# Making the first layer's shift and scale by quarters of the channels

## The reference

```python
c_act = jax.nn.silu(c)
for l in range(DEPTH):                                   # DEPTH = 2
    mod = c_act @ w_ada[l] + b_ada[l]                    # (1, 3 * 2048)
    shift, scale, gate = jnp.split(mod, 3, axis=-1)
    h = _rmsnorm(x, norm_g[l]) * (1.0 + scale[:, None, :]) + shift[:, None, :]
    z = h @ w_in[l]                                      # 13 pieces of 512 columns
    ...                                                  # mixers, gates
    x = x + gate[:, None, :] * (concat @ w_out[l])
...                                                      # pooling layer, latent attention layer
```

## Time and profile before

| | |
|---|---|
| median of 3 runs | 2161.24 us (2158.2 to 2162.18) |
| profiled execution, its own time | 2157.21 us |
| span of the profiled execution | 2155.4 us |
| TensorE busy | 2087.6 us, 97% of the span |
| VectorE, ScalarE busy | 1513.2 us, 948.2 us |
| DMA | 511.40 MB, mean 237 GB/s |

### The profile page before, as it was taken

How to read it: one execution, slowest core, us unless ns; L and a number is a source line. 1 busy time by engine, 2 the same in 40 slices (tenths; PEclk the granted TensorE clock), 3 DMA queues, 4 the chain that set the end, 5 groups by cost and what they waited for, 6 DMA issues and landing times.

```text
span 2155.4 us, 32744 instructions
## 1 busy us (share of the span) xinstructions
PE 2087.6 (97%) x13530; PEld 1762.3 (82%) x13530; DVE 1513.2 (70%) x1923; ACT 948.2 (44%) x1318; POOL 201.7 (9%) x386
## 2 busy tenths in 40 slices
PE   5889999999999999999999999999999999999997
PEld 3668878887889878886987878787778999988876
DVE  0355879886765888865897868678788886455554
ACT  2234555553535555555632222223247553444452
POOL 2211110110011111110010100000100000000000
PEclk9999999999999999999999999999999999999999
DMA  9998887779697787777576646555887778322253
GB/s 381 383 332 304 276 315 245 251 270 343 201 356 265 263 274 264 256 270 275 184 275 201 212 146 196 163 174 166 299 289 256 233 255 265 103 70 77 78 191 131
DMA packets 215484, 511.40 MB, mean 237 GB/s; under 512 B 19728, under 2 KB 26096, under 8 KB 213680
## 3 DMA queue, kind: packets, MB, share of 16 engines
q1 hardware_dynamic: 155536, 297.83, 40.8%
q0 software_dynamic: 54464, 201.76, 26.9%
q10 hardware_dynamic: 5344, 9.84, 1.5%
HBM read 500.93 MB, written 8.43 MB: 236 GB/s over the span
## 4 chain that ended last, share of the span: by engine, by line
PE 70%; DVE 7%; DMA 4%; ACT 2%; issue 1%; DVEq 0%; ACTq 0%
PE ps L821 21%; PE ps L822 20%; PE ps L823 20%; DMA w_raw<-in_w_out 3%; DVE ada_acc L2306 2%; PE ps L877 2%; PE ps L1500 1%; DVE wl L2406 1%; DVE wl L2413 1%; PE ps L1492 1%; ACT wh L1604 1%; PE ps L1483 1%; DMA ada_raw<-in_ada_w 0%; PE ps L1199 0%; PE ps L1019 0%
## 5 line engine op out<-in xcount | busy, mean ns | idle before, releaser
L2413 DVE TENSOR_TENSOR wl<-w_raw,wh 128x1024 fp32r<-128x1024 f32 x280 | 334.7, 1221 | 197.9 <-ACT wh L1604 197.1
L1604 ACT ACTIVATE wh<-w_raw 128x1024 fp32r<-128x1024 f32 x280 | 291.6, 1056 | 346.9 <-PE ps L823 234.4
L1656 ACT ACTIVATE wh<-w_raw 128x1024 fp32r<-128x1024 f32 x220 | 230.5, 1057 | 403.2 <-PE ps L823 346.9
L821 PE MATMUL ps<-hh,wh 128*128 128x256 f32 x1280 | 371.5, 290 | 9.8 <-DVE hl L2474 9.0
L822 PE MATMUL ps<-hh,wl 128*128 128x256 f32 x1280 | 361.2, 282 | 0.0
L823 PE MATMUL ps<-hl,wh 128*128 128x256 f32 x1280 | 360.7, 282 | 0.0
L2406 DVE TENSOR_TENSOR wl<-w_raw,wh 128x1024 fp32r<-128x1024 f32 x220 | 266.8, 1221 | 130.6 <-ACT wh L1656 130.2
L821 PE MATMUL ps<-act_hl,wh 128*128 128x256 f32 (+1 forms) x1056 | 351.4, 333 | 2.9 <-DVE wl L2406 2.9
L822 PE MATMUL ps<-act_hl,wl 128*128 128x256 f32 (+1 forms) x1056 | 348.6, 330 | 0.0
L823 PE MATMUL ps<-act_hl,wh 128*128 128x256 f32 (+1 forms) x1056 | 348.4, 330 | 0.0
L2306 DVE SCALAR_TENSOR_TENSOR ada_acc<-ada_raw,cpad,ada_acc 128x1024 f32<-128x1024 f32 x263 | 329.5, 1280 | 13.5 <-DMA ada_raw<-in_ada_w 11.7
(11 more groups left out here) (414 smaller groups left out, 3113.0 us busy)
## 6 DMA issues: line engine op xcount, KB each, us to landing
ada_raw<-in_ada_w POOLq DMA_DIRECT2D x272, 512.0 KB, 5.3
w_raw<-in_w_in SPq DMA_DIRECT2D x208, 512.0 KB, 5.3
w_raw<-in_pool_in SPq DMA_DIRECT2D x72, 512.0 KB, 4.7
w_raw<-in_w_out SPq DMA_DIRECT2D x64, 512.0 KB, 7.6
w_raw<-in_mla_in SPq DMA_DIRECT2D x56, 512.0 KB, 4.8
ada_fourth<-in_ada_w POOLq DMA_DIRECT2D x48, 512.0 KB, 6.6
w_raw<-in_pool_out SPq DMA_DIRECT2D x48, 512.0 KB, 5.5
w_raw<-in_mla_out SPq DMA_DIRECT2D x32, 512.0 KB, 3.8
```

What stands on the lines that cost most here:

```text
L821: pe.matmul(dst, ah, bh, start=start, stop=False, skip_group_check=True)
L1604: act.activation(wh[:, g % RING, :], w_raw[:, g % RING, :], ACT.Copy).then_inc(w_hi, 1)
L1656: act.activation(as_raw(g, wh[:, r, :]), raw_of(g), ACT.Copy).then_inc(w_hi, 1)
L2413: dve.tensor_tensor(wl[:, g % RING, :], w_raw[:, g % RING, :], wh[:, g % RING, :].bitcast(F32), ALU.subtract).then_inc(w_lo, 1)
```

## The change

The early blocks become 128 rows by 512 columns of shift and the same 512 columns of scale, so sixteen blocks finish both for a quarter of the channels. The order of the first three pieces follows the quarters: two slots each of pieces 0 and 1 for the first quarter (g = 0 to 3), two each for the second (4 to 7), four of piece 2 (8 to 11), two of each piece for the third (12 to 17) and for the fourth (18 to 23). The early blocks are spread anew between the slots, SyncE loads only blocks 1 to 15 of them, its weight loads get gates on the number of used blocks (`EARLY_GATE`), all eight `turn_x` stand in the first sixteen blocks, VectorE's first sixteen later blocks move from steps 0 to 12 into steps 5 to 12, TensorE's from steps 4 to 10 into steps 5 to 10, and `tab` and the slabs are loaded behind slots 22 and 26.

```diff
-SLAB_SLOTS = ({20: 2, 24: 2}, {116: 2, 120: 2})
+SLAB_SLOTS = ({22: 2, 26: 2}, {116: 2, 120: 2})
-EARLY_PIECES = (0, 2, 1, 3)
+EARLY_Q = GRP // P
+EARLY_FROM = (0, 4, 12, 18)
+EARLY_SPLIT = (4, 4, 4, 0)
+EARLY_TILL = ((22, 24, 26, 28), (37, 38, 39, 40, 41, 42, 43, 44), (53, 54, 55, 56, 57, 58))
+EARLY_GATE = {1: 8, 2: 14, 4: 24, 6: 30, 12: 40, 14: 46, 18: 56, 20: 62}
...
-SLOTS_OF = [[(p, s) for s0 in (0, HALF) for p in range(3) for s in range(s0, s0 + HALF)]
+SLOTS_OF = [[(p, s) for p in range(2) for s in (0, 1)] + [(p, s) for p in range(2) for s in (2, 3)]
+            + [(2, s) for s in range(4)] + [(p, s) for s0 in (4, 6) for p in range(3) for s in (s0, s0 + 1)]
...
-EARLY_STEPS = [RING, 2]
+EARLY_STEPS = [RING + 1, 2]
...
-ADA_DVE = [{**spread(0, 0, [1] * 8 + [2, 1, 2, 1, 2]), **spread(1, 13, [1, 2, 1, 2, 2, 2] + [1] * 6),
+ADA_DVE = [{**spread(0, 5, [2] * 8), **spread(1, 13, [1, 2, 1, 2, 2, 2] + [1] * 6),
...
-ADA_PE = [{**spread(2, 4, [1, 2, 2, 2, 3, 3, 3]), **spread(4, 12, [4] + [3] * 4), **spread(5, 19, [2] * 8)},
+ADA_PE = [{**spread(2, 5, [2, 2, 3, 3, 3, 3]), **spread(4, 12, [4] + [3] * 4), **spread(5, 19, [2] * 8)},
...
-            eng.dma_start(early_bufs[r], ada_k[:, 0, i % ADA_SLOTS, piece * ADA_W:(piece + 1) * ADA_W]
-                          ).then_inc(early_here(i)[0], 16)
+            eng.dma_start(early_bufs[r].rearrange("p (j n) -> p j n", j=2),
+                          ada_k[:, 0, i % ADA_SLOTS, 0:2, at:at + GRP]).then_inc(early_here(i)[0], 16)
...
-            for i in range(1, 2 * ADA_SLOTS, 2):
+            for i in range(1, ADA_SLOTS, 2):
                 early_load(sp, i)
...
-                    if l == 0 and g in (1, 3 * HALF):
-                        sp.wait_ge(ada_pe, 52 if g > 1 else 29)
+                    if l == 0 and g in EARLY_GATE:
+                        sp.wait_ge(ada_pe, EARLY_GATE[g])
...
             for n in range(4, 8):
                 turn_x(n)
-                early_slots(2 * n, 2 * n + 2)
-            ada_turn(0, 6)
-            early_slots(ADA_SLOTS, ADA_SLOTS + 6)
-            pe.wait_ge(ada_row, 5)
+                early_slots(n + 4, n + 5)
+            pe.wait_ge(ada_row, 4)
             for n in range(4):
                 turn_x(n)
-                early_slots(ADA_SLOTS + 6 + 2 * n, ADA_SLOTS + 8 + 2 * n)
-            early_slots(2 * ADA_SLOTS - 2, 2 * ADA_SLOTS)
-            ada_turn(1, 7)
+                early_slots(n + 12, n + 13)
...
+                        if l == 0 and g in EARLY_FROM:
+                            n = EARLY_FROM.index(g)
+                            if n:
+                                early_slots(EARLY_TILL[n - 1][-1], ADA_SLOTS * (n + 1))
+                            ada_turn(n, 6 + n % 2)
+                            early_slots(ADA_SLOTS * (n + 1), ADA_SLOTS * (n + 1) + EARLY_SPLIT[n])
...
-            rows_out(0, ADA_SLOTS, 6)
             for n in range(4):
                 act.wait_ge(xT_ps, n + 1)
                 act.activation(xT_up[:, n * 512:(n + 1) * 512], ps[:, n, :], ACT.Copy).then_inc(ada_row, 1)
...
+            for q in range(4):
+                first, till = EARLY_FROM[q], (*EARLY_FROM, 20)[q + 1]
+                for g in (first, first + 1):
+                    his(g // RING, 0, 0, (g % RING,))
+                rows_out(q, ADA_SLOTS * (q + 1), 6 + q % 2)
+                h_his(0, 2 * q, 2 * q + 2)
+                for g in range(first + 2, till):
+                    his(g // RING, 0, 0, (g % RING,))
...
+            for q in range(4):
+                first, till = EARLY_FROM[q], (*EARLY_FROM, 20)[q + 1]
+                for g in (first, first + 1):
+                    lo(g // RING, g % RING, 0)
+                early_result(q)
+                dve.wait_ge(mod_ok, q + 1)
+                h_of_layer(0, 2 * q, 2 * q + 2)
+                for g in range(first + 2, till):
+                    lo(g // RING, g % RING, 0)
```

More of the change, by code:

```diff
@@ L74 @@
 SLOTS_A = STEPS * RING
-HALF = BLK // 2
-SLOTS_OF = [[(p, s) for s0 in (0, HALF) for p in range(3) for s in range(s0, s0 + HALF)]
+SLOTS_OF = [[(p, s) for p in range(2) for s in (0, 1)] + [(p, s) for p in range(2) for s in (2, 3)]
+            + [(2, s) for s in range(4)] + [(p, s) for s0 in (4, 6) for p in range(3) for s in (s0, s0 + 1)]
             + [(p, s) for p in range(3, NP_) for s in range(BLK)],
             [(p, s) for p in range(NP_) for s in range(BLK)]]
-OUT_AT = [{(max(i for i, (q, _) in enumerate(order) if q == p) + 1) // RING: p for p in range(NP_)}
-          for order in SLOTS_OF]
-EARLY_STEPS = [RING, 2]
+LAST_SLOT = [[max(i for i, (q, _) in enumerate(order) if q == p) for p in range(NP_)] for order in SLOTS_OF]
+OUT_AT = [[[p for p in range(NP_) if (last[p] + 1) // RING == t] for t in range(2 * NP_ + 1)] + [[]] * (2 * D // GRP)
+          for last in LAST_SLOT]
+EARLY_STEPS = [RING + 1, 2]
 NA0, RET0, FFT0, CONV0, LN0 = 7, 16, 19, 10, 24
@@ L610, in early_here @@
         def early_here(i):
-            r, half = i % EARLY_RING, 2 * ADA_SLOTS
+            r, half = i % EARLY_RING, ADA_SLOTS
             if r % 2 and i >= half:
@@ L778, in ada_load_more @@
                                ).then_inc(ada_landed[m % ADA_RING], 16)
-            for i in range(0, 2 * ADA_SLOTS, 2):
+            for i in range(0, ADA_SLOTS, 2):
                 early_load(pool, i)
-            for i in range(2 * ADA_SLOTS, ADA_EARLY):
+            for i in range(ADA_SLOTS, ADA_EARLY):
                 early_load(pool, i)
@@ L1111, in _ @@
                         slot(g, l * SLOTS_A + g, PIECES[p][2], bank0, SLOT_K * s, s == 0, s == BLK - 1, hh, hl)
[L1112 to L1117, removed]
+                        if l == 0 and g < EARLY_FROM[3]:
+                            n = max(n for n in range(3) if EARLY_FROM[n] <= g)
+                            done = (ADA_SLOTS * (n + 1) + EARLY_SPLIT[n], *EARLY_TILL[n])
+                            early_slots(done[g - EARLY_FROM[n]], done[g - EARLY_FROM[n] + 1])
                 ada_first(SMALL_STEP)
@@ L2486, in early_result @@
             def early_result(n):
-                kind, half = n % 2, n // 2
-                ada_turned(n, (0,), kind, half, cl("b_ada", 16 * kind + 8 * half, 8), cl("norm_g", 8 * half, 8), 6 + n % 2)
+                dve.wait_ge(ada_cols, n + 1)
+                turned = ps[:, 6 + n % 2, 256:512].rearrange("p (h q r) -> p r q h", h=2, r=32)
+                for kind in range(2):
+                    at = 16 * kind + EARLY_Q * n
+                    ins = dve.tensor_tensor(mod[:, 0, at:at + EARLY_Q].rearrange("p (q h) -> p q h", h=2),
+                                            turned[:, 0, 2 * kind:2 * kind + 2, :],
+                                            cl("b_ada", at, EARLY_Q).rearrange("p (q h) -> p q h", h=2), ALU.add)
+                ins.then_inc(ada_read, 1)
+                dve.wait_ge(ada_read, n + 1)
+                m = mod[:, 0:1, 16 + EARLY_Q * n:16 + EARLY_Q * (n + 1)]
+                dve.scalar_tensor_tensor(m, m, 1.0, bc(cl("norm_g", EARLY_Q * n, EARLY_Q), 1), ALU.add, ALU.mult
+                                         ).then_inc(mod_ok, 1)
             rstd_of_x(0)
@@ L2691, in _ @@
                         ada_in_layer(t)
-                    if t in OUT_AT[l]:
-                        pieces_fin(OUT_AT[l][t])
+                    for p in OUT_AT[l][t]:
+                        pieces_fin(p)
                     mixers_first(t)
@@ L2772, in _ @@
             lo_of(POOL0 + 5)
-            dve.wait_ge(mod_ok, 6)
+            dve.wait_ge(mod_ok, 8)
             dve.wait_ge(ada_read, 4 + 6 * DEPTH)
```

43 lines of the change are left out of this document (11 added, 32 removed).

## The result

The change made the kernel slower, by 0.2%: 2164.97 us (2159.6 to 2172.46, 22 runs) against 2159.97 us (2158.2 to 2165.31, 22 runs), a ratio of 1.0024 [1.0016, 1.0033]. The forecast was 2152.2 us, in 2145 to 2159. The profiled execution took 2162.57 us by its own time, span 2160.8; before 2157.2 and 2155.4.

A forecast was written before the change was run, and what follows sets the result against it. It took the head (before 160 us) as fed by DMA and the rest as paced by TensorE. Slot 24 wins 12.8 us, less 0.6 and 3.5, is 8.7, taken as 9: median 2152.2 us, range 2145 to 2159.

The forecast's parts named there:

- The head: Stretch before 160 us, fed by DMA: slot 24 was to start at 151.5 us instead of 164.3, 12.8 us won.
- First quarter: Up to slot 0: sixteen early blocks suffice instead of 32, so slot 0 starts at 43.3 us, 17 us earlier.
- with equal runs I expect equal shares: GpSimd's and SyncE's queues while both full: bytes near ratio 1 instead of 2.1, weights sooner, early blocks later.
- The second and fourth quarter's chains: Row copy and turn: 1.0 us before slot 4 (68 us); uncovered chain of 4.5 us before slot 18 (131.5 us).
- 2 us for the short runs: Early loads in runs of 2 KB instead of 4 KB: 3% more time on early bytes, 2 us by slot 12.
- Step 7: TensorE's third block there is loaded only after VectorE's block behind the softmax work: stall 2.8 to 4.5 us, taken 3.5.
- So they are hidden as work: VectorE's five blocks moved into later steps, 6.4 us of work, cost no time as VectorE is busy 69 of 100 us.
- A rest paced by TensorE, to which any time won in the head passes on one to one: From 160 us on TensorE has no idle time, DMA slack (0.83); everything behind step 12 should keep its length.
- the slower rival: Step 7's stall repeats in steps 8, 9 and 10: 6 us slower, 2167 us; chance 0.1.
- DMA eats the gain: Early blocks in one queue at half bandwidth make quarters end late: 0 to 4 us won, 2157 to 2161 us; chance 0.2.
- The faster rival: TensorE never waits for DMA in the head and step 7 is covered: 16 us won, 2145 us; chance 0.2.

The follow-up runs named there:

- e1: Changed kernel with row copy and shift and scale put ahead of the weights in ScalarE's and VectorE's order; 2162.86 us, 1.0010.
- e13: Changed kernel with the first 24 weight slots read in runs of 4 KB (other weights, so other products); 2163.71 us, 1.0010.
- e14: Kernel before the change with the first 24 weight slots read in runs of 4 KB (other weights); 2157.72 us, 0.9982.
- e4: Kernel before the change with its early loads read in two runs of 2 KB instead of one of 4 KB; 2169.64 us, 1.0043.
- e5: Changed kernel with layer 0's `w_ada` laid out by quarters, so early loads have runs of 4 KB again; 2159.43 us, 0.9991.
- e2: Changed kernel with TensorE's third adaLN block of step 7 moved to step 10; 2163.46 us, 1.0012.
- e7: e2's edit on the changed kernel, and VectorE's sixteen blocks spread from step 4 on with one in step 11; 2165.82 us, 1.0024.
- e11: Changed kernel with the edits of e1 and e5 together, schedule of later blocks as changed; 2160.27 us, 0.9998.
- e8: Changed kernel with the edits of e1, e5 and e7 together; 2156.2 us, 0.9979.
- e9: e1 with sixteen later adaLN loads cut to 256 of their 1024 columns (part of the gate made from wrong blocks); 0.9959.
- e3: Changed kernel with each early load issued as two loads of 128x512; 2168.11 us, 1.0033.
- e12: Changed kernel with the edits of e1, e5 and e2 together; 2155.85 us, 0.9979.

## Why the prediction was wrong

*The direction* failed, in two places. The head did not bring the gain (slot 24 at 160.9 us, not 151.5), because weights land later than priced and a row copy stands behind them. And the frame did not hold, that what slot 24 wins passes on to the end: with e1's order slot 24 started within 0.3 us of the forecast, and the kernel was still no faster than before. Step by step:

- *First quarter, "both weights land ... rounded by 38.1 us, row copied 38.5".* The step that failed first. Rounded at 39.89 and 43.78, row at 44.75: 6.3 us late. One part is "with equal runs I expect equal shares". The trace has packets of 4096 B for GpSimd's loads whatever the runs, and of 2048 B for SyncE's, so in 34 to 43 us SyncE's queue got 35% of the bytes (1.21 of 3.47 MB). With equal bytes (e13) the row is copied at 42.15, so this is 2.6 us. The other 3.7 us stay with equal shares: there the weights are still 2.63 us apart, and the first is rounded at 38.56, where the forecast had the second land near 37. The price of a weight beside a full queue of early blocks was too low. The row itself could have been copied at 36.9 (e1), had nothing stood ahead of it. The Trainium skill (DMA: Bandwidth & Descriptors, Queues, rings and completion order) has engines serve their queues in turn by packets. The 631 to 636 packets agree with it; it was applied to the runs of the source, which are not the packets. The 2.1 bytes to one of the earlier trace rows, which the prediction took for this rule at work, could not show it: e14 doubled the weights' packets and the ratio was 2.3.
- *The second and fourth quarter's chains* had the same error: waits for the row of 2.05 and 4.18 us. Slot 18, forecast at 131.5, came at 141.1. Of the 9.4 us by which slot 24 missed, e1's order alone gives back 9.1, by two profiles whose heads can differ by a few us.
- *"2 us for the short runs".* Mis-sized. Their price alone is 9.9 us in the kernel before (e4), and e5 gives back 0.33%, 7.1 us. I read 390 against 379 GB/s off two queues that share the same engines, as if each had its own rate; with DMA full, 34 to 43 us has 411 GB/s before and 386 after. The Trainium skill (DMA: Bandwidth & Descriptors, Specifications) takes 512 B as enough for line rate and would make it nothing. The measurement decides against it.
- *Step 7.* Right in mechanism and place: VectorE's blocks ran from 182.05 us, the load was issued at 183.63, and `ada_raw` landed late at 188.02. Mis-sized: 5.0 us, not 3.5. The wait there is 2.60 us and the granted clock behind it 0.61 (188 to 192 us), which I did not charge here although I had in the head. e2 removes it.
- *"So they are hidden as work".* Not in step 12, where TensorE waits for two blocks and 1.8 us are lost; e7, with one VectorE block in step 11 instead of two, has 0.1.
- *"A rest paced by TensorE, to which any time won in the head passes on one to one".* The error that decides. The share of 0.83 over 100 us hid that in the kernel before DMA is full from 160 to 170 us (1.00) and at 0.91 from 170 to 180; the slack begins at 180 (0.46 up to 190). e1 won 12.5 us and kept 0.5: it lost 5.8 us between slots 24 and 28, where the forecast charged 0.6, and 4.8 in step 7, where it charged 3.5.
- *The rivals.* By its time the slower rival was nearest (6 us slower; 5.0 measured), which is luck: its stalls in steps 8 to 10 did not come, and from slot 32 to 48 the changed kernel loses nothing. "DMA eats the gain" had early blocks late where weights were. The faster rival needed a TensorE that never waits for DMA in the head, and from 120 to 160 us it was busy 32.73 of 40 us.
- *Two slips in the sum.* The terms given for slot 0 add up to 42.7 and not 43.3 us, and those for slot 18 to 131.2 and not 131.5.

How the parts add: in the two profiles, 3.4 us are won at slot 24, 0.8 lost by slot 28, 5.0 in step 7, 1.8 in step 12 and 1.2 behind slot 52, which makes +5.4 us at the end; the forecast had 12.8 won, 0.6 and 3.5 lost, and nothing more. The order of weights and rows holds 9.1 us of slot 24's start, but made good it returns only 3.0 us of the total (by the ratios, 1.0024 to 1.0010). The layout returns 7.1 us (to 0.9991), order and layout 5.6 (to 0.9998), both with step 7's schedule 9.7 (to 0.9979); the interval of each ratio is about 2 us to either side, so that of a difference is about 3. Layout alone and order with layout can't be told apart by it. That order and layout don't add up is what a limit of bytes just behind slot 24 would give: e11 has slot 24 at -11.2 and slot 28 at -8.3, and loses 6.6 us more in step 7. The profile of e1 is one of its two fastest runs (2156.91 us; the median is 2162.86), so its gains may flatter it. Not settled: a wait of 2.6 us for `wl` near slot 120 that stands in the profiles of e8, e9 and e11, shorter (1.0 to 2.0 us) in those of e2, e3, e5, e7 and e13, and not in those of before, the changed kernel, e1 and e12. What decides it is not known.

## What to carry to other kernels

A gain in a stretch fed by DMA is kept only if the stretch behind it has its bytes, and its schedule of loads, ready as much sooner: look at DMA in slices as short as the gain, not at a mean over 100 us. When a load's layout changes, work out anew which queue gets which share, from the packets that the trace lists and in a stretch where neither queue is held by its consumer; the ratio in a stretch where one is held only tells what is consumed. And where a short operation releases the rest (a row copy), put nothing ahead of it in its engine's order that waits for a transfer.

## What the hardware showed

- GpSimd's loads with two runs of 2 KB, and those split in two loads of 2 KB rows, still go in packets of 4096 B; SyncE's loads with runs of 2 KB go in packets of 2048 B. A packet of 4096 B in GpSimd's queue took 173 ns in the changed kernel and 167 before (60 to 100 us), one of 2048 B in SyncE's 90 and 86.
- Two queues that both had work were served about packet for packet: 631 to 636 (34 to 43 us) and 827 to 833 (78 to 90 us) in the changed kernel, 654 to 657 (e5) and 507 to 513 (e13) in 34 to 43 us. Two runs do not fit in 34 to 43 us: e3, with 613 to 776 packets, and e4, with 371 to 1091. In e4 SyncE's early loads took 8.7 to 11.1 us to land and GpSimd's 6.7 to 9.6. It may be that GpSimd's queue was empty part of the time in both; that was not tested.
- Issuing an early load took GpSimd 0.72 us with two runs for each row, and 0.53 us with one.
